# Both feed-forward output projections by Strassen's method, one level, with the weight sums made by accumulating DMAs

## The reference, cut to what matters

```python
D_MODEL, SEQ, DEPTH, FFN_HIDDEN = 1024, 512, 2, 2816
def conv_ffn(x, w_up, b_up, w_dw, b_dw, w_down, b_down):
    h = x @ w_up + b_up                        # 512 x 5632
    h = causal_depthwise_conv(h, w_dw, b_dw)   # width 3
    g, val = jnp.split(h, 2, axis=-1)
    return (jax.nn.silu(g) * val) @ w_down + b_down
for i in range(DEPTH):
    y = conformer_conv_module(...) if i % 2 == 0 else chunked_spatial_gating(...)
    x = layer_norm(DEEPNORM_ALPHA * x + y, norm1_g[i], norm1_b[i])
    y = conv_ffn(x, ...)
    x = layer_norm(DEEPNORM_ALPHA * x + y, norm2_g[i], norm2_b[i])
```

## Time and profile before

| | |
|---|---|
| median of three runs | 1077.75 us |
| the profiled execution | 1077.49 us |
| its span, first to last instruction | 1075.5 us |
| TensorE busy, share of the span | 98% |
| VectorE, ScalarE, GpSimd busy | 65%, 42%, 11% |
| mean granted TensorE clock | 0.998 |
| HBM traffic over the span | 102 GB/s |

### The profile page before, as it was taken

The page is one execution under the profiler, slowest core; times in us unless marked ns, Lnnn a source line. Parts: engine busy times, 40 slices in busy tenths (PEclk is TensorE's granted clock), DMA queues, the critical chain, the costliest instruction groups (busy, mean ns, idle before and its releaser), DMA issues.

```text
span 1075.5 us, 14271 instructions
## 1 busy us (share of the span) xinstructions
PE 1058.2 (98%) x4935; PEld 882.2 (82%) x4935; DVE 701.5 (65%) x955; ACT 456.3 (42%) x683; POOL 120.7 (11%) x129
## 2 busy tenths in 40 slices
PE   9999989999999999999999999999999999999997
PEld 7778768988888888888888888898888888888885
DVE  7999976596767676523274676659776767652325
ACT  7999935343434343311143342344343434331111
POOL 1798800000000000000010110000000000000001
PEclk9999999999999999999999999999999999999999
DMA  9578324023222323432226232303232323242211
GB/s 339 157 184 196 98 61 135 22 90 106 97 98 89 106 80 115 176 99 98 98 99 214 79 117 80 118 20 112 84 116 79 112 83 101 94 157 98 98 40 78
DMA packets 34102, 118.87 MB, mean 111 GB/s; under 512 B 3728, under 2 KB 4752, under 8 KB 34064
## 3 DMA queue, kind: packets, MB, share of 16 engines
q1 hardware_dynamic: 29744, 102.63, 28.1%
q0 software_dynamic: 2304, 8.39, 4.1%
q10 hardware_dynamic: 2016, 7.34, 1.9%
HBM read 107.86 MB, written 2.10 MB: 102 GB/s over the span
## 4 chain that ended last, share of the span: by engine, by line
PE 86%; ACT 9%; DVE 2%; issue 1%; DMA 1%; SPq 1%; POOL 0%; DVEq 0%; POOLq 0%; ACTq 0%
PE ps L1045 16%; PE ps L1043 16%; PE ps L1044 16%; PE ps L1053 12%; PE ps L1055 11%; PE ps L1054 11%; ACT prods L516 3%; ACT diagh L496 1%; ACT wh L457 1%; ACT diagl L497 1%; PE ps L1191 1%; ACT wl L459 1%; DMA raw<-d_weights 1%; DVE ps L790 1%; ACT gsum L516 0%
## 5 line engine op out<-in xcount | busy, mean ns | idle before, releaser
L1043 PE MATMUL ps<-xh,wh 128*128 128x512 f32 x816 | 317.8, 389 | 0.4 <-DMA wl<-raw 0.4
L1044 PE MATMUL ps<-xl,wh 128*128 128x512 f32 x816 | 317.5, 389 | 0.0
L1045 PE MATMUL ps<-xh,wl 128*128 128x512 f32 x816 | 317.5, 389 | 0.0
L721 DVE TENSOR_TENSOR wl<-raw,wh 128x1024 fp32r<-128x1024 f32 x72 | 88.1, 1227 | 164.9 <-ACT wh L457 164.9
L1043 PEld LDWEIGHTS ps<-xh,wh 128*128 128x128 f32 x816 | 153.2, 188 | 32.8 <-DMA wl<-raw 0.8
L1044 PEld LDWEIGHTS ps<-xl,wh 128*128 128x128 f32 x816 | 153.2, 188 | 32.0
L1045 PEld LDWEIGHTS ps<-xh,wl 128*128 128x128 f32 x816 | 153.2, 188 | 31.9
L457 ACT ACTIVATE wh<-raw 128x1024 fp32r<-128x1024 f32 x84 | 88.3, 1055 | 176.7 <-PE ps L1055 171.1
L1053 PE MATMUL ps<-wh,hh 128*128 128x512 f32 x352 | 137.1, 389 | 0.0
L1055 PE MATMUL ps<-wh,hl 128*128 128x512 f32 x352 | 136.9, 389 | 0.0
L1054 PE MATMUL ps<-wl,hh 128*128 128x512 f32 x352 | 136.9, 389 | 0.0
(11 more groups left out here) (139 smaller groups left out, 1471.1 us busy)
## 6 DMA issues: line engine op xcount, KB each, us to landing
raw<-d_weights SPq DMA_DIRECT2D x178, 512.0 KB, 3.3
wl<-raw POOLq DMA_DIRECT2D x12, 512.0 KB, 6.5
xraw<-d_x_fm SPq DMA_DIRECT2D x8, 256.0 KB, 6.0
res<-d_x_tm SPq DMA_DIRECT2D x4, 512.0 KB, 7.6
res<-brow POOLq DMA_DIRECT2D x4, 512.0 KB, 4.5
brow<-d_rows ACTq DMA_DIRECT2D x3, 512.0 KB, 3.9
grow<-d_rows ACTq DMA_DIRECT2D x3, 512.0 KB, 5.8
brow_n<-d_rows ACTq DMA_DIRECT2D x3, 512.0 KB, 7.5
```

The lines of the kernel that those rows point to most:

```text
L721: eng.tensor_tensor(l, raw[:, u % RAW, :], h.bitcast(f32), ALU.subtract).then_inc(w_lo, 1)
L1043: eng.matmul(ps[:, bank, cols], a, xh[:, k, cols], start=(k == 0), stop=False)
L1044: eng.matmul(ps[:, bank, cols], a, xl[:, k, cols], start=False, stop=False)
L1045: mm = eng.matmul(ps[:, bank, cols], b, xh[:, k, cols], start=False, stop=(k == KD - 1))
```

## The change

The hidden matrix A (512 x 2816) is cut in two halves of positions and two halves of the hidden width (even and odd tiles of 128), the weight matrix B in the same halves of the hidden width and in two halves of output channels. The four quarter products per output quarter (8 in all) are replaced by 7 products of sums of quarters. In the program's names, with `made` holding the float32 quarters and `parts` their high and low parts:

- P1 = A11 B11, P2 = A12 B21 (the plain quarters, 11 units); P5 = (A21-A22) T1, P6 = S2 T2 (11 units of weight sums); P3 = S4 B22, P7 = V7 T3 (11 units); P4 = A22 T4 (6 units). `n5`, `s2`, `s4`, `v7` are the sums of hidden quarters.
- A unit now has 12 matmuls (a tile, two blocks of 128 positions, 3 parts, for each of two products), and there are 39 units a layer (`DOWN`) instead of 22. The 28 after the first 11 are read from `summed_d`, a tensor in HBM that the kernel fills.
- `summed_weights` fills it, a layer at a time, by 100 DMAs of 128 x 512 values (256 KB) from HBM to HBM, issued by GpSimd from the end of the norm before `ffn_up`: 56 copies, 44 accumulating. SP waits for all of them before it loads the first summed unit.
- `summed_hidden` (GpSimd) makes the sums of hidden quarters, 24 additions a layer, behind the DMAs in its order; ACT and DVE split them (`hi_of`, `lo_of_part`) between the weight units. `shared_sums` (GpSimd) makes six additions on `res`.
- DVE adds the products to `res` in twelve pieces of 128 x 512 (`add`). The second half of the positions is finished by P4, the norm of the first half runs beside it. The low parts of the first four units of `U_GV` go from DVE to GpSimd (`early_lo`).
- The loop of SP is written out. Some buffers are laid out anew.

```diff
+DOWN = 3 * KQ + (KQ + 1) // 2
+SUMMED = DOWN - KQ
+BY_POOL = range(U_GV, U_GV + RING)
+GROUP = 2
+NG = (KQ + GROUP - 1) // GROUP
...
     @block.sync
+        for u in range(2 * RAW, UNITS):
             eng.wait_ge(*lo_of(u - RAW))
+            for layer in range(DEPTH):
+                if u == U_DOWN[layer] + KQ:
+                    eng.wait_ge(w_copied, 16 * 3 * KQ * (layer + 1))
+                    eng.wait_ge(w_t1, 16 * KQ * (layer + 1))
+                    eng.wait_ge(w_t2, 16 * KQ * (layer + 1))
+                    eng.wait_ge(w_sums, 16 * 2 * KQ * (layer + 1))
             load(u % RAW, u)
...
     @block.gpsimd
+        def summed_weights(layer):
+            w1 = weights_d[first_raw(layer):first_raw(layer) + KQ]
+            w2 = weights_d[first_raw(layer) + KQ:first_raw(layer) + KH]
+            to = summed_d[layer]
+            for i in range(KQ):
+                eng.dma_start(to[i, :, first], w1[i, :, first]).then_inc(w_copied, 16)
+                eng.dma_start(to[KQ + i, :, second], w2[i, :, first]).then_inc(w_copied, 16)
+                eng.dma_start(to[KQ + i, :, first], w2[i, :, second]).then_inc(w_copied, 16)
+                eng.wait_ge(w_copied, 16 * 3 * (layer * KQ + i + 1))
+            for i in range(KQ):
+                eng.dma_start(to[i, :, first], w2[i, :, first], accum_op=ALU.add).then_inc(w_t1, 16)
+                eng.dma_start(to[KQ + i, :, second], w2[i, :, second], accum_op=ALU.add).then_inc(w_sums, 16)
+                eng.wait_ge(w_sums, 16 * (2 * layer * KQ + i + 1))
+                eng.wait_ge(w_t1, 16 * (layer * KQ + i + 1))
+            for i in range(KQ):
+                eng.dma_start(to[i, :, second], to[i, :, first]).then_inc(w_t2_copied, 16)
+            eng.wait_ge(w_t2_copied, 16 * KQ * (layer + 1))
+            for i in range(KQ):
+                eng.dma_start(to[i, :, second], w2[i, :, second], accum_op=ALU.add).then_inc(w_t2, 16)
+                eng.wait_ge(w_t2, 16 * (layer * KQ + i + 1))
...
+        def summed_hidden(layer):
+            for g in range(NG):
+                c, done = group(g), 4 * (layer * NG + g)
+                eng.wait_ge(w_used, U_DOWN[layer] + c.stop)
+                eng.tensor_tensor(n5[:, c, :], a21[:, c, :], a22[:, c, :], ALU.subtract).then_inc(a_sum, 1)
...
+        for t in range(NT):
+            norm_root(1 + t, t + 1, t)
+        summed_weights(0)
+        summed_hidden(0)
+        shared_sums(0)
+        for t in range(NT):
+            if t == 2:
+                early_lo(U_GV)
+                early_lo(U_GV + 1)
+                early_lo(U_GV + 2)
+            if t == NT - 1:
+                early_lo(U_GV + 3)
+            norm_root(1 + NT + t, NT + t + 1, t)
...
     @block.vector
+        def ffn_down(layer, n, u0):
+            for i in range(3 * KQ):
+                if i == KQ:
+                    eng.wait_ge(w_used, u0 + KQ)
+                    add(0, 0, p1, 1.0)
+                    add(1, 0, p1 + 1, 1.0)
...
+                los([u0 + LEAD + i])
...
+                g, odd = divmod(i - 5, 2)
+                if 0 <= g < NG and not odd:
+                    lo_of_part(n5l, n5, n5h, g, first_parts(layer, g))
+                    lo_of_part(s2l, s2, s2h, g, first_parts(layer, g) + 1)
+                g, odd = divmod(i - KQ - 3, 2)
+                if 0 <= g < NG and not odd:
+                    lo_of_part(s4l, s4, s4h, g, later_parts(layer, g))
+                    lo_of_part(v7l, v7, v7h, g, later_parts(layer, g) + 1)
+                    lo_of_part(a22l, a22, a22h, g, later_parts(layer, g) + 2)
```

More of the change, by code:

```diff
@@ L674, in _ @@
             if h == 0:
+                row(glb[:, :], R_GLB, gm_in)
                 his(range(U_GU, U_GU + LEAD))
@@ L716, in los @@
             for u in units:
-                if u < UNITS:
+                if u < UNITS and u not in BY_POOL:
                     wait_split(eng, u)
@@ new lines, in product @@
+            def product(u, c, bank, h, l, i, first, last):
+                w_h, w_l = split_at(u)
+                cols = slice(c * HALF, (c + 1) * HALF)
+                for t in range(NT // 2):
+                    s_h, s_l = h[:, i, t * P:(t + 1) * P], l[:, i, t * P:(t + 1) * P]
+                    eng.matmul(ps[:, bank + t, :], s_h, w_h[:, cols], start=first, stop=False)
+                    eng.matmul(ps[:, bank + t, :], s_h, w_l[:, cols], start=False, stop=False)
+                    mm = eng.matmul(ps[:, bank + t, :], s_l, w_h[:, cols], start=False, stop=last)
+                return mm
@@ new lines, in fourth @@
+            def fourth(i, tiles):
+                u = u_down + 3 * KQ + i // 2
+                h, l = split_at(u)
+                cols = slice(i % 2 * HALF, (i % 2 + 1) * HALF)
+                if tiles[0] == 0:
+                    eng.wait_ge(*lo_of(u))
+                    eng.wait_ge(a_lo, later_parts(layer, i // GROUP) + 3)
+                for t in tiles:
+                    s_h, s_l = a22h[:, i, t * P:(t + 1) * P], a22l[:, i, t * P:(t + 1) * P]
+                    eng.matmul(ps[:, p4 + t, :], s_h, h[:, cols], start=(i == 0), stop=False)
+                    eng.matmul(ps[:, p4 + t, :], s_h, l[:, cols], start=False, stop=False)
+                    mm = eng.matmul(ps[:, p4 + t, :], s_l, h[:, cols], start=False, stop=(i == KQ - 1))
+                return mm
@@ new lines, in ffn @@
+            for i in range(KQ):
+                third(i)
+                if i < KQ - 2:
+                    seventh(i)
+            seventh(KQ - 2)
+            seventh(KQ - 1)
+            eng.wait_ge(q_ok, 4 * (layer + 1))
+            by_k = 2 * (FOURTH - LAST)
+            for i in range(by_k):
+                mm = fourth(i, (0, 1))
+                if i % 2:
+                    mm.then_inc(w_used, 1)
+            for i in range(by_k, KQ):
+                mm = fourth(i, (0,))
+            mm.then_inc(blk, 1)
```

326 lines of the change are left out of this document (276 added, 50 removed).

## The result

The changed kernel takes 1168.66 us (median of 4 runs, 1158.46 to 1173.09), the kernel before 1077.53 beside it. The ratio is **1.083** (95% interval 1.079 to 1.087): 8% slower, where I forecast 1.1% faster. 1168.66 lies outside my range of 1050 to 1110.

A forecast was written before the change was run, and what follows sets the result against it. TensorE bounds the kernel, busy 98% of the span, so time is matmuls times pitch; -29.9 + 2.4 + 10 + 2 + 4 + 0 = -11.5 from 1077.5 gives 1066.0 us, range 1050 to 1110.

The forecast's parts named there:

- The weight sums: DMA chain beside `ffn_up`: 221 us a layer with 249 us free, so 0 cost to the kernel.
- lower bound of 179: Shortest estimate in us of a layer's weight-sum chain, from DMA rows of the earlier trace, none from HBM to HBM.
- The upper bound, 297: Longest estimate in us of a layer's weight-sum chain: half the rate for HBM data and 1 us more a round.
- Rival L: Weight sums late, at SP's wait ahead of unit 11 and POOL's first addition; slower than before; chance 0.27.
- its formula: Late sums: 1066 us plus, once a layer, each microsecond of chain past 249; 1108 at 270, 1162 at 297.
- break-even of 255: Chain length in us a layer at which late weight sums use up the forecast gain of 11.5 us.
- Matmuls removed: PE: 462 matmuls a layer instead of 528, 132 fewer in all at 0.227 us each, -29.9 us.
- Start of each projection: PE waits 1.2 us for the low part of the fourth weight unit, twice: +2.4 us.
- DVE in P5 and P6: GpSimd's hidden additions and DVE's work partly exclude each other: +5 us a layer, +10, bounds 0 and 18 a layer.
- rival W: Port held for whole instructions, P5 and P6: 18 us a layer instead of 5, kernel 1092 us, slower; chance 0.10.
- `res` additions: Six GpSimd additions in the stage after P5 and P6 meet DVE likewise: +1 us a layer, +2 (0 to 4).
- Entry to the gMLP: Layer 0 only: low parts of the first four gMLP units, now on POOL, come late for PE: +4 us (0 to 8).

The follow-up runs named there:

- experiment 1: The change with one wait per phase of the weight sums instead of one per round, same DMAs: 1077.39 us, ratio 0.9993 to the kernel before.
- experiment 4: The kernel before plus the change's 200 weight-sum DMAs, a wait in each round, nobody waiting for the result: 1081.64 us, ratio 1.0035.
- runs 1 to 3: The change with one wait per phase, 1077.39 us; with no weight sums, 1072.37; without sums and with constant fills for GpSimd's hidden additions, 1056.72.

## Why the prediction was wrong

**The weight sums, "0 for the sum, since 28 us are spare": the step that failed.** The chain took 293 us instead of 221, and was on the path for 44 and 43 us. With nothing beside it, it takes 256, already past the 249 that were free. So the lower bound of 179 was 77 us under what the chain takes alone. A round with one accumulating DMA is 4.3 us instead of 3.2; if each of the 46 waited rounds is longer by these 1.1 us, that is, by this estimate, 51 of the 77. The other 26 are what further DMAs in a round or a phase add: 2.2 us for a second accumulating one instead of 1.33, and 0.95 for a copy from HBM to HBM, where the earlier trace rows, from two transfers out of SBUF, gave 0.6. The 0.9 us a round that I added "for HBM as target and for the loads" is almost what the loads alone cost, 0.8; it was a good figure for one of the two things that it was to cover.

The upper bound, 297, lies above the 293 of the fastest run, but hardly above the others. The median run is 10.2 us longer, 5 us a layer if all of it is the chain's, which gives 298. The bound was also added up wrong: half the rate and 1 us more a round, as the prediction words it, give 6.5, 8.2, 5.5, 5.5 and 33, some 315 us. The mistake was to compare the estimate, not the bound, with what is free. A chain equally likely anywhere from 179 to 297 would be past the break-even of 255 with a chance of 0.36 instead of 0.27; the larger error is that the range reached down to 179, from rows of which none showed a DMA from HBM to HBM.

**Rival L** came as written in place (SP ahead of unit 11, POOL's first addition) and sign. Its price, 1152.9 by its formula for the two chains, is 5.6 us under the profiled run, and that this is so near is partly luck. The formula starts from 1066, where experiment 1 has 1077; and the lateness costs 1158.46 - 1076.98 = 81.5 us between the two profiled runs, less than the 86.9 of the formula. PE's waits for the weight units are 76.7 us of it (88.5 against 11.8). The fall of the clock that I ruled out ("it should stay at its high level") belongs to it: in 498 to 535 us, 84 matmuls at 0.30 instead of 0.227 us are 6 us. The other runs lie up to 15 us higher, some 7 us a layer; whether their chains are longer, no trace of them shows. The chain in experiment 4 took 300 us.

**Matmuls removed, -29.9:** right. 4803 matmuls, 132 fewer. With the constant fills, where little else is left of the change, the profiled run is 20.9 us faster than that of the kernel before: -29.9, 4.9 of waits of PE, and some 4 more, of which the end after the last matmul is 1.0 (7.5 to 8.5 us); the rest is open.

**Start of each projection, 1.2 x 2:** the place is right, the fourth unit; the wait is 0.6 to 0.9 a layer.

**DVE in P5 and P6, 5 a layer, and `res`:** the mechanism of rival W with the size between. The additions cost 15.7 us for both layers, where I had 10 (bounds 0 to 36 with W). "About 0.95 us of an addition" was read from one subtraction that had lost 0.25 us because it began late in a POOL addition. An instruction holds the other up for most of its length, as W says; it costs less than W says, because only three pairs of units a layer come at 7.84 us or a little less, not five at 9.0. Of the `res` additions (I had 2) only this is known, that it makes no difference which engine has them.

**Entry to the gMLP, +4:** 2.00 + 0.6 us of waits, though another thing waits: not the gMLP's units on POOL, but the last unit of the fourth product on DVE, behind them.

**Missing:** 3.7 us at the last line of the kernels with the 200 DMAs, the change among them.

By the medians of runs 1 to 3 and of the kernel before beside them, the change with its sums in time is -21.5 + 15.7 + 5.0 = -0.8, nothing against the kernel before. My -11.5 missed 3.7 in the exclusion (15.7 for 10 + 2), 5.0 in traffic and end, and 2.0 in the small terms (29.9 - 21.5 = 8.4 for 2.4 + 4). So even without L the forecast would have been too good by 11 us.

## What to carry to other kernels

Work that is "hidden beside" a stage needs its length bounded from above, and that bound compared with the stage: here 118 us of uncertainty stood beside 28 us of room. A chain of dependent small DMAs costs its round trips; one wait per phase instead of one per round halved it alone (256 to 132 us) without changing a byte, and should be the first form written. And an addition handed to GpSimd to relieve VectorE is no relief while VectorE works on two SBUF tensors: the 48 additions cost 15.7 us on GpSimd and some 4 (15.7 - 11.5, an estimate over two sets of runs) in VectorE's own queue.

## What the runs showed of the hardware that I had not expected

- A waited round of one accumulating DMA from HBM to HBM, 256 KB, takes 4.3 us alone and 5.2 beside loads; with all in flight 1.5 to 1.8 and 2.2 us each.
- DMA engines at 0.72 in place of 0.28 for 240 us cost PE nothing, nor did 0.98 for 25 us (experiment 4).
- An operation of VectorE that reads PSUM and one SBUF tensor is not held up by GpSimd (0.68 us inside an addition of GpSimd, among operations stretched by 1 us). Operations on two SBUF tensors are, but for some 0.1 us each.
- Kernels with 200 more DMAs on GpSimd's queue spend 3.4 to 3.7 us more at the last line; with 134 or 4 more they do not. The cause is open.
